# A two-block transformer kernel on one core: fewer extra matmuls, gates computed earlier, and one filler product moved

## The chip, the cores and the metric

The kernel runs on one core of one Trainium2 chip. The metric is the device time of one execution in microseconds (us), here the median of three runs.

## What is computed

256 tokens of width 1024 go through three layers, all in float32. The first two are a block with modulated norms: layer 0 mixes by Fourier transform and windowed attention, layer 1 by pooling, and each ends with a gated MLP of 22 hidden tiles of 128. The third layer is what the middle part of the change touches:

```python
h = rmsnorm(x, norm_mix)
(dn_qkv, dn_z, dn_b, dn_a, ns_q, ns_kc, ns_vc, ns_ks, ns_vs, ns_kw, ns_vw, ns_gate,
 gate_dn, gate_nsa) = split(h @ w_in)
...
beta = sigmoid(b_logit)
g = -exp(a_log) * softplus(a_logit + dt_bias)          # decay of the delta rule, per head
gates = sigmoid(gate_logits)                            # three branches of attention
...
mix = sigmoid(gate_dn) * (o_dn @ w_proj_dn) + sigmoid(gate_nsa) * (o_ns @ w_proj_nsa)
x = x + mix @ w_out
x = x + square(relu(rmsnorm(x, norm_mlp) @ w_up)) @ w_down
```

o_dn comes from the gated delta rule (8 heads, chunks of 64, a triangular solve for each), o_ns from attention over compressed, selected and windowed keys (16 heads of 64).

## The kernel before

**A product.** Every big product is `product(unit, xh, xl, ...)`. Weights and activations are split in a high part (float32r) and a low part, and each of the 8 slices of 128 rows of the contraction takes three matmuls of 256 columns: high by high (L562), high by low (L563), low by high (L564). One unit of weights (128 x 1024) is 24 matmuls, that is, eight such triples.

**Splitting the weights.** SyncE loads chunks into a ring. For each unit ScalarE (ACT) writes the high part (L1375, waiting for TensorE to be done with the unit four before), and VectorE (DVE) writes the low part (L1889, waiting for ACT's). Both do this inside their own copy of the order of work, up to three units ahead of TensorE (PE). In f1, `next_weights` takes the unit and the split of the unit ahead comes at the end of the same step.

**Order.** Each engine has its program written out by hand, and goes through it strictly in order. Waits are on named steps: `pe.at(step)`, `act.at(step)`, `dve.at(step)`.

**settle(x)** (L646) is one matmul of 128 x 64 on data already in place, into a scratch bank; its result is used by nobody. It stands at the end of each `opening`, at some steps j of the up phase of layers 0 and 1 (22 steps of two units), of the last MLP's up phase (32 steps of one unit, the first two in the opening), and at a few other places.

**f1** (third layer, projections for attention). PE: f1(12) to f1(15); `gates()`, a product for all small gate columns; f1(0); `gates_turned()`, two transposes; f1(1); f1(2) with `f1_squares(1)` behind its product (L580, which waits for ACT's squares L1627 of f1(0) and f1(1)); f1(3) with `f1_spread(1)` behind it (L953, which waits for DVE's reciprocal L2178 in its f1(3)); hidden(0), 64 matmuls for compressed keys; f1(4) and so on. On ACT, f1(j) is: for even j from 2 the deviation (a Sqrt, L1609), the square L1627, the copy L1629, the split of a unit ahead. On DVE it is: for odd j from 3 the reciprocal, and the split. `blocks(e)` on DVE (L2213) builds the input of hidden(e); `gates()` on DVE stands behind blocks(0), copies the turned gates to gt (L2148), and adds the bias to dt (L2150, L2151). `gates2()` on ACT (L1593 to L1599) waits for gt and dt and does two Tanh, Abs and two Exp; on DVE (L2157 to L2163) it finishes beta, gate and dt1. `gates3()` on ACT is a Ln of dt1 (L1603); on DVE it finishes gg.

**f2 and delta.** f2 is 24 products, and behind product s stand the steps `f2_later(s)` of the two before: DVE convolves along the tokens (L2400, L2403), ACT takes a Tanh (L1739), DVE multiplies (conv, L2391), PE transposes (L1143), ACT copies (L1730). So `f2_later(24)` and `f2_later(25)` are left over behind the last product. Behind `pe.note("f2")` and its likes the memory of the attention part is used anew, and the other engines wait there for each other. Then comes the delta rule: `decay(hd)` on PE (L1192 to L1194) waits for DVE's sources (L2443, L2444), ACT takes Exp (L1785), GpSimd masks (L2639), PE does `products(hd)` (L1200 to L1204), DVE multiplies (L2450 to L2458). 16 independent fillers (`fill()`; the first eight are one product each, the others two) stand between these steps. Behind the loop over hd come `level_first` (L1219) and the levels of the triangular solve.

Of the kernel before, what the change touches and what calls it, by code (L numbers as in the profile page):

```python
# [322 lines left out]
def program(nc, a):  # L323
    ctx = ExitStack()
    with ctx:
# [23 lines left out]
        pe, act, dve, pool = Mark(sem("s_pe")), Mark(sem("s_act")), Mark(sem("s_dve")), Mark(sem("s_pool"))  # L349
# [197 lines left out]
        def tensor_program(te):  # L547
# [280 lines left out]
            def swiglu(layer, norm, after):  # L828
                F.past(EXTRA[2][0])
                later = iter(ADA_LATER[layer])  # L830

                def ada_later():
                    of, _ = next(later)
                    F.used(F.raw(f"adaT{of}"))
                for j in range(NH0):
                    ps = take(RG, ("up", layer, j), (dve, ("prod", layer, j)))
                    if j == 0:
                        opening(f"w13_{layer}", norm, [(ps[:, 0:T], True), (ps[:, T:2 * T], False)], [("up", layer, 0, e) for e in range(2)])
                    for e in range(2 if j else 0):
                        u, _ = F.take(f"w13_{layer}")  # L840
                        product(u, xh, xl, norm, ps[:, e * T:(e + 1) * T]).then_inc(*pe.up(("up", layer, j, e), ("unit", u)))
                    if ADA_UP[layer](j):
                        ada_later()
                    if j in (1, 4, 8, 12, 16):
                        settle(xh)
                pe.note(("x", norm))
                n = 0
                for j in range(8):
                    ps = take(RG, ("down", layer, j), (dve, ("h", after, j)))
                    for k in range(NH0):  # L850
                        if n % 8 == 0:
                            u, _ = F.take(f"w2_{layer}")
                            _, hi, lo = unit_of(u)
                            P.wait_ge(*lo_done(u))
                        P.wait_ge(*dve.at("hid", layer, k))
                        c = slice((n % 8) * 128, (n % 8 + 1) * 128)
                        end = mm3(ps[:, 0:T], hi[:, c], lo[:, c], hh[:, k, :], hl[:, k, :], k == 0, k == NH0 - 1)
                        steps = [("unit", u)] * (n % 8 == 7) + [("down", layer, j)] * (k == NH0 - 1)
                        if steps:
                            end.then_inc(*pe.up(*steps))  # L860
                        if k == NH0 - 1 and j in (0, 3):
                            settle(hh)
                        if n % 8 == 7:
                            F.done(u)
                            if n % 16 == 15 and ADA_DOWN[layer](n // 16):
                                ada_later()
                        n += 1
                if layer == 0:
                    mean_square_rest(after)
                else:  # L870
                    mean_squares_last()
                pe.note(("hid", layer))
                if layer == 0:
                    spread(after)
# [253 lines left out]
            def f2_later(s):  # L1128

                if not 0 <= s - 2 < 24:  # L1130
                    return
                j = F2[s - 2]
                if j < 16 and j % 2:
                    ps = take(RAS, ("qks", j), (dve, ("qkv", j)))
                    for e in range(2):
                        P.wait_ge(*act.at("qksq", j - 1 + e))
                        end = column_sums(lambda t: ps[:, 2 * t + e:2 * t + e + 1], sq[:, j % 8 - 1 + e, :], 0, ones[:, 0:1])
                    end.then_inc(*pe.up(("qks", j)))
                if j >= 16:
                    P.wait_ge(*dve.at("conv", j))  # L1140
                    ps = take(RAS, ("vt", j), (act, ("vt", j)))
                    for t in range(2):
                        end = te.transpose(ps[:, t * 128:(t + 1) * 128], sq[:, j % 8, t * 128:(t + 1) * 128], ident)  # L1143
                    end.then_inc(*pe.up(("vt", j)))
# [3 lines left out]
            for s, j in enumerate(F2):  # L1148
                if STEPS2[s]:
                    attn_head(step)  # L1150
                u, _ = F.take("f2")
                ps = take(RGS, ("f2", j), (dve, ("f2", j)))
                product(u, xh, xl, "mix2", ps[:, 0:T]).then_inc(*pe.up(("f2", j), ("unit", u)))
                f2_later(s)
                if STEPS2[s]:
                    attn_tail(step)
                    step += 1


            def fill_z(j):  # L1160
# [13 lines left out]
            def fill(n=1):  # L1174
                for _ in range(n):
                    j = next(fillers)
                    if j < 8:
                        fill_z(j)
                    else:
                        gated("gn", j - 8, onh, onl, "on", RO)  # L1180


            fill()
            f2_later(24)
            f2_later(25)
            pe.note("f2")

            def decay(hd):
                ps = take(RA, ("decay", hd), (act, ("decay", hd)))
                P.wait_ge(*dve.at("rg", hd))  # L1190
# [16 lines left out]
            for hd in range(8):  # L1207
                if hd < 7:
                    decay(hd + 1)
                products(hd)  # L1210
                if hd in (1, 3, 5):
                    fill()

            def level_first(n):
# [117 lines left out]
            for j in range(2, NH2):  # L1332
                u, _ = F.take("up")
                ps = take(RG, ("mup", j), (act, ("mup", j)))
                product(u, xh, xl, "mlp2", ps[:, 0:T]).then_inc(*pe.up(("mup", j), ("unit", u)))
                if j in (2, 5, 9, 14, 20, 26):
                    settle(xh)
            n = 0
            for j in range(8):
# [17 lines left out]
        def scalar_program(sc):  # L1357
# [233 lines left out]
            def gates2():  # L1591
                A.wait_ge(*dve.at("gt"))
                sc.activation(beta[:, :, :], gt[:, :, 0:8], ACT.Tanh, scale=0.5).then_inc(*act.up("beta"))  # L1593
                sc.activation(gate[:, :, :], gt[:, :, 16:64], ACT.Tanh, scale=0.5).then_inc(*act.up("gate"))
                A.wait_ge(*dve.at("dt"))
                sc.activation(gw[:, 0, :, :], gt[:, :, 8:16], ACT.Abs).then_inc(*act.up())
                A.wait_ge(*act.now())
                sc.activation(gw[:, 0, :, :], gw[:, 0, :, :], ACT.Exp, scale=-1.0).then_inc(*act.up("dtexp"))
                sc.activation(ea[:, :], C("alog"), ACT.Exp).then_inc(*act.up("ea"))  # L1599

            def gates3():
                A.wait_ge(*dve.at("dt1"))
                sc.activation(gw[:, 1, :, :], gw[:, 1, :, :], ACT.Ln).then_inc(*act.up("dtln"))  # L1603
# [87 lines left out]
            for j in (12, 13, 14, 15):  # L1691
                f1(j)
            gates()
            for j in range(4):
                f1(j)
            gates2()
            gates3()
            hidden(0)
            f1(4)
            compressed(0)  # L1700
# [70 lines left out]
            def fill(n=1):  # L1771
                for _ in range(n):
                    j = next(fillers)
                    if j >= 8:
                        gated("gn", j - 8)
                        continue
                    weights("f3")
                    A.wait_ge(*pe.at("zz", j))
                    sc.activation(temp(("zz", j), (dve, ("zz", j))), ps_of(("zz", j))[:, 0:T], ACT.Tanh, scale=0.5).then_inc(*act.up(("zz", j)))
# [4 lines left out]
                    A.wait_ge(*dve.at("W", hd - 2))  # L1784
                sc.activation(Ebuf[:, hd % 2, :], ps_of(("decay", hd))[:, 0:384], ACT.Exp).then_inc(*act.up(("decay", hd)))  # L1785

            fill()
            decay(0)
            for hd in range(8):
                if hd < 7:  # L1790
                    decay(hd + 1)
                if hd in (1, 3, 5):
                    fill()
            fill()
            fill()
# [77 lines left out]
        def vector_program(ve):  # L1873
# [314 lines left out]
            def f1(j):  # L2188
                ahead = next_weights("f1")
                if j < 12 and j % 2 and j > 1:  # L2190
                    f1_inverse(j - 2)
                if j < 12 and j % 2 == 0 and j > 2:
                    unit_rms(j - 3)
                if j == 6:
                    compressed_keys()
                if j == 10:
                    compressed_values()
                split(ahead)
# [134 lines left out]
            f1(0)  # L2333
            blocks(0)
            gates()
            for j in (1, 2, 3):
                f1(j)
            gates2()
            gates3()
            V.wait_ge(*dve.at("qg"))  # L2340
            for half in range(2):
                F.used(F.raw("cw1"))
# [117 lines left out]

            sources(0)
            sources(1)
            fill()
            for hd in range(8):
                if hd < 6:
                    sources(hd + 2)
                products(hd)
                if hd in (1, 3, 5):
                    fill()

            fill()
# [467 lines left out]
```

## Time and profile before

| | us |
|---|---|
| median of three runs | 1208.61 |
| lowest and highest | 1206.75, 1209.2 |
| the profiled execution's own time | 1209.2 |
| its span, first to last instruction | 1207.4 |
| mean granted TensorE clock in it | 0.983 of full speed |
| PE, DVE, ACT, GpSimd busy | 1149.0, 814.4, 589.9, 81.8 |

The times of the profile count from the first instruction. A row of a timeline gives start, duration, engine, line, operation and how many were merged, and in brackets how long the engine was idle ahead of it and who released it. Matmuls overlap: the pace is read from start to start, not from the duration.

### The profile page before, as it was taken

The page shows a single profiled execution, that of the slowest core. Times are in us where ns is not written, and L with a number is a line of the kernel's source. Part 1 is how long each engine was busy: PE and PEld are TensorE (multiplying, and loading weights), DVE is VectorE, ACT ScalarE, POOL GpSimd, SP SyncE. Part 2 cuts the span into 40 slices and gives each one's busy share as a digit, 9 for nine tenths or more (in the row PEclk, how much of TensorE's full clock was granted, in tenths as well). Part 3 has the DMA queues.
Part 4 walks back from the last instruction along what each step waited for, and adds up shares of the span by engine and source line. Part 5 has one row for each costly group of instructions (what it writes and reads, how often), then busy time and mean ns, then how long its engine had stood idle before and what let it go on. Part 6 is the DMA issues. An engine that isn't in the chain of part 4 may idle for free.

```text
span 1207.4 us, 24317 instructions
## 1 busy us (share of the span) xinstructions
PE 1149.0 (95%) x10429; PEld 1092.4 (90%) x10429; DVE 814.4 (67%) x1490; ACT 589.9 (49%) x1084; POOL 81.8 (7%) x100
## 2 busy tenths in 40 slices
PE   5888789999998999999989999999999999999999
PEld 2687689999997999999989888888999999999999
DVE  3783668898886767555674678787664665877543
ACT  2434556454544545454465557653234445655432
POOL 0000110000011000001100111112600001000000
PEclk9789999999999999999998999999999999999999
DMA  9751548889884555751653232232123464855520
GB/s 388 291 207 60 215 170 329 334 340 349 320 328 174 222 222 223 255 187 43 246 175 105 106 105 80 97 105 71 38 72 106 157 211 159 323 198 185 208 84 14
DMA packets 32363, 226.41 MB, mean 188 GB/s; under 512 B 3584, under 2 KB 4736, under 8 KB 5120
## 3 DMA queue, kind: packets, MB, share of 16 engines
q1 hardware_dynamic: 30528, 221.20, 49.1%
q10 hardware_dynamic: 1728, 3.67, 0.8%
q8 instruction: 82, 1.34, 0.4%
q14 instruction: 25, 0.20, 0.1%
HBM read 223.80 MB, written 1.05 MB: 186 GB/s over the span
## 4 chain that ended last, share of the span: by engine, by line
PE 86%; DVE 8%; ACT 4%; DMA 1%; issue 1%; POOL 0%; SPq 0%; DVEq 0%; POOLq 0%
PE bank L562 23%; PE bank L563 22%; PE bank L564 22%; PE bank L1041 2%; PE bank L687 2%; DVE sb_tmp L1915 1%; DVE sb_ring L1930 1%; DVE sb_wlo L1889 1%; PE bank L580 1%; PE bank L1032 1%; PE bank L1063 1%; DMA sb_ring<-in_ada 1%; PE bank L590 1%; PE bank L600 1%; PE bank L1229 1%; PE bank L1247 1%
## 5 line engine op out<-in xcount | busy, mean ns | idle before, releaser
L562 PE MATMUL bank<-sb_xh,sb_whi 128*128 128x256 f32 x1488 | 422.9, 284 | 9.0 <-DVE sb_wlo L1889 6.7
L563 PE MATMUL bank<-sb_xl,sb_whi 128*128 128x256 f32 x1488 | 414.3, 278 | 0.0
L564 PE MATMUL bank<-sb_xh,sb_wlo 128*128 128x256 f32 x1488 | 414.3, 278 | 0.0
L1889 DVE TENSOR_TENSOR sb_wlo<-sb_ring,sb_whi 128x1024 fp32r<-128x1024 f32 (+1 forms) x197 | 239.1, 1220 | 138.5 <-ACT sb_whi L1375 138.1
L562 PEld LDWEIGHTS bank<-sb_xh,sb_whi 128*128 128x128 f32 x1488 | 281.6, 189 | 17.6 <-issue 12.8
L563 PEld LDWEIGHTS bank<-sb_xl,sb_whi 128*128 128x128 f32 x1488 | 282.2, 190 | 0.1
L564 PEld LDWEIGHTS bank<-sb_xh,sb_wlo 128*128 128x128 f32 x1488 | 281.7, 189 | 0.0
L1375 ACT ACTIVATE sb_whi<-sb_ring 128x1024 fp32r<-128x1024 f32 (+1 forms) x197 | 206.7, 1053 | 88.7 <-PE bank L564 81.3
L1889 DVE TENSOR_TENSOR sb_wlo<-sb_more,sb_whi 128x1024 fp32r<-128x1024 f32 x108 | 131.0, 1222 | 64.8 <-ACT sb_whi L1375 64.8
L562 PE MATMUL bank<-sb_hh,sb_whi 128*128 128x256 f32 x608 | 168.4, 277 | 0.0
L564 PE MATMUL bank<-sb_hh,sb_wlo 128*128 128x256 f32 x608 | 167.8, 276 | 0.0
L563 PE MATMUL bank<-sb_hl,sb_whi 128*128 128x256 f32 x608 | 167.8, 276 | 0.0
L1375 ACT ACTIVATE sb_whi<-sb_more 128x1024 fp32r<-128x1024 f32 x108 | 114.0, 1057 | 66.2 <-PE bank L564 56.1
L563 PEld LDWEIGHTS bank<-sb_hl,sb_whi 128*128 128x128 f32 x608 | 114.2, 188 | 0.0
L562 PEld LDWEIGHTS bank<-sb_hh,sb_whi 128*128 128x128 f32 x608 | 114.1, 188 | 0.0
L564 PEld LDWEIGHTS bank<-sb_hh,sb_wlo 128*128 128x128 f32 x608 | 114.1, 188 | 0.0
L1930 DVE CUSTOM_DVE_ANT_0 sb_ring<-sb_ring,sb_cB,sb_col 128x1024 f32<-128x1024 f32 x46 | 58.0, 1299 | 0.0
L1536 ACT ACTIVATE sb_tmp<-bank 128x256 f32<-128x256 f32 x44 | 16.9, 384 | 66.2 <-PE bank L564 66.2
L1397 ACT ACTIVATE sb_sq<-sb_h 128x256 f32<-128x256 f32 x48 | 19.2, 415 | 58.9 <-DVE sb_h L1944 54.2
L2600 POOL TENSOR_TENSOR sb_sq<-sb_sq 128x256 f32<-128x256 f32 x24 | 19.2, 801 | 367.2 <-ACT sb_sq L1397 366.3
L1930 DVE CUSTOM_DVE_ANT_0 sb_more<-sb_more,sb_cB,sb_col 128x1024 f32<-128x1024 f32 x34 | 42.7, 1292 | 0.0
L1667 ACT ACTIVATE sb_ss<-sb_ss,sb_st 128x128 f32<-128x128 f32 x64 | 28.1, 442 | 7.2 <-DVE sb_st L2303 7.2
(378 smaller groups left out, 1845.6 us busy)
## 6 DMA issues: line engine op xcount, KB each, us to landing
sb_more<-in_w SPq DMA_DIRECT2D x34, 1024.0 KB, 6.7
sb_ring<-in_w SPq DMA_DIRECT2D x32, 1024.0 KB, 6.0
sb_ring<-in_adaT SPq DMA_DIRECT2D x26, 1024.0 KB, 7.6
sb_ring<-in_f SPq DMA_DIRECT2D x22, 1024.0 KB, 5.0
sb_more<-in_adaT SPq DMA_DIRECT2D x18, 1024.0 KB, 9.5
sb_ring<-in_gn SPq DMA_DIRECT2D x8, 1024.0 KB, 4.9
sb_ring<-in_gd SPq DMA_DIRECT2D x8, 1024.0 KB, 4.9
sb_ring<-in_up SPq DMA_DIRECT2D x8, 1024.0 KB, 5.9
```

The source lines that it names most:

```text
L562: te.matmul(out, wh, rh, start=start, stop=False, skip_group_check=skip)
L563: te.matmul(out, wh, rl, start=False, stop=False, skip_group_check=skip)
L564: return te.matmul(out, wl, rh, start=False, stop=stop, skip_group_check=skip)
L687: end = te.matmul(ps_of(("row", e))[0:2, :], csil[:, k, :], w[:, o:o + 512], start=k == 0, stop=k == KT - 1)
L1041: end = te.matmul(ps[:, k * 128:(k + 1) * 128], ss[:, i % 3, u, k * 128:(k + 1) * 128], dg2[:, i % 2, 2 * u + (k > 0), :], start=True, sto ...
L1375: sc.activation(hi, x, ACT.Copy).then_inc(*hi_done.up(n))
L1397: sc.activation(sq[:, k, :], src[:, k, :], ACT.Square).then_inc(*act.up(("sq", norm, k)))
L1536: sc.activation(temp(("silu", layer, j), (dve, ("hid", layer, j))), ps_of(("up", layer, j))[:, 0:T], ACT.Silu).then_inc(*act.up(("silu", l ...
L1667: sc.activation(p, p, ACT.Exp, bias=x[:, 1, u, t:t + 1], scale=slope((2 * aa + u) * 4 + r), accum_out=x[:, 2, u, t:t + 1]).then_inc(*act.u ...
L1889: ve.tensor_tensor(lo, x, hi.bitcast(F32), ALU.subtract).then_inc(*lo_dve.up(n))
L1930: ve.tensor_tensor_reduce(out=x, in0=x, in1=cB[:, 0, :], scale=1.0, scalar=C(f"ab{layer}", jj, jj + 1), op0=ALU.mult, op1=ALU.add, accum_o ...
L2600: gp.tensor_tensor(sq[:, 0, :], sq[:, 0, :], sq[:, k, :], ALU.add).then_inc(*pool.up(("sum", norm, k)))
```

## The change

Four edits:

- PE leaves out the settle at j = 1, 4 and 12 in layers 0 and 1, and in the last up phase stands one at j = 11 and 21 in place of j = 2, 5, 9, 14, 20, 26.
- On all three engines the first filler, ahead of `decay(0)`, is taken out, and there is one more at hd = 7 of the delta loop. On PE the left-over `f2_later(24)` and `(25)` so follow the last f2 product directly.
- On ACT gates2 moves from behind f1(3) to behind f1(0), and gates3 to behind f1(1).
- On DVE gates2 moves to behind f1(1), and gates3 to behind f1(2).

```diff
@@ tensor_program, swiglu
-                    if j in (1, 4, 8, 12, 16):
+                    if j in (8, 16):
                         settle(xh)
@@ tensor_program, behind the f2 loop
+            f2_later(24)
+            f2_later(25)
+            pe.note("f2")
...
-            fill()
-            f2_later(24)
-            f2_later(25)
-            pe.note("f2")
@@ tensor_program, delta loop (the same in scalar_program and vector_program, which also lose the fill() ahead)
                 products(hd)
-                if hd in (1, 3, 5):
+                if hd % 2:
                     fill()
@@ tensor_program, last MLP
-                if j in (2, 5, 9, 14, 20, 26):
+                if j in (11, 21):
                     settle(xh)
@@ scalar_program, f1
             gates()
-            for j in range(4):
+            f1(0)
+            gates2()
+            f1(1)
+            gates3()
+            for j in (2, 3):
                 f1(j)
-            gates2()
-            gates3()
             hidden(0)
@@ vector_program, f1
             gates()
-            for j in (1, 2, 3):
-                f1(j)
+            f1(1)
             gates2()
+            f1(2)
             gates3()
+            f1(3)
```

## Rows read from the trace of the kernel before

**Rows 1.** The page, busy time, share of the span and instructions of each engine.

```profile
PE 1149.0 (95%) x10429; PEld 1092.4 (90%) x10429; DVE 814.4 (67%) x1490; ACT 589.9 (49%) x1084; POOL 81.8 (7%) x100
```

**Rows 2.** Waits of TensorE: line, releaser, us in total, times, longest.

```profile
PE bank L953 <- DVE sb_hdev L2178: 4.7, 4, 1.9
...
PE bank L1219 <- DVE sb_qk L2475: 0.2, 1, 0.2
```

**Rows 3.** Timeline of TensorE, around the settle at j = 1 in layer 0.

```profile
198.47 0.19 PE L649 MATMUL bank<-sb_xh 128*128 128x64 f32 x1
...
199.29 0.28 PE L562 MATMUL bank<-sb_xh,sb_whi 128*128 128x256 f32 x1
...
209.49 0.28 PE L562 MATMUL bank<-sb_xh,sb_whi 128*128 128x256 f32 x1
```

**Rows 4.** Timeline of TensorE, first and last of 91 matmuls without a break.

```profile
945.42 0.28 PE L562 MATMUL bank<-sb_xh,sb_whi 128*128 128x256 f32 x1
...
956.02 0.28 PE L562 MATMUL bank<-sb_onh,sb_whi 128*128 128x256 f32 x1
```

**Rows 5.** Timeline of VectorE, 600 to 615 us.

```profile
603.65 4.11 DVE L2213 TENSOR_TENSOR sb_bk<-sb_kcv,sb_col 64x240 f32<-64x240 f32 x8
...
608.20 0.16 DVE L2151 TENSOR_TENSOR sb_gt<-sb_gt,sb_col 128x8 f32<-128x8 f32 x1
...
610.68 0.20 DVE L2178 RECIPROCAL sb_hdev<-sb_hdev 128x8 f32<-128x8 f32 x1
612.13 1.23 DVE L1889 TENSOR_TENSOR sb_wlo<-sb_ring,sb_whi 128x1024 fp32r<-128x1024 f32 x1 [1.26 <-ACT sb_whi L1375]
...
614.19 0.17 DVE L2161 TENSOR_SCALAR sb_gw<-sb_gw 128x16 f32<-128x16 f32 x1
```

**Rows 6.** Timeline of ScalarE, 600 to 615 us.

```profile
601.41 1.06 ACT L1375 ACTIVATE sb_whi<-sb_qk 128x1024 fp32r<-128x1024 f32 x1
...
607.57 0.27 ACT L1609 ACTIVATE sb_hdev<-bank,sb_col 128x8 f32<-128x8 f32 x1 [1.90 <-PE bank L580]
607.73 0.38 ACT L1627 ACTIVATE sb_sq<-bank 128x256 f32<-128x256 f32 x1
...
608.26 1.07 ACT L1375 ACTIVATE sb_whi<-sb_ring 128x1024 fp32r<-128x1024 f32 x1
...
612.12 1.28 ACT L1593 ACT_TABLE_LOAD   x1
613.41 0.22 ACT L1593 ACTIVATE sb_beta<-sb_gt 128x16 f32<-128x16 f32 x1
...
614.06 0.19 ACT L1599 ACTIVATE sb_ea<-sb_col 128x8 f32<-128x8 f32 x1
```

**Rows 7.** Timeline of TensorE, 606 to 612 us.

```profile
606.58 0.95 PE L580 MATMUL bank<-sb_con,sb_sq 128*128 128x2 f32 x8
...
610.93 1.09 PE L953 MATMUL bank<-sb_con,sb_hdev 128*64 128x128 f32 x16 [0.47 <-DVE sb_hdev L2178]
```

**Rows 8.** TensorE by windows: us, busy (instructions), granted clock, DMA share, GB/s.

```profile
818.40:821.80 3.40, 2.93 (x10) 0.51 0.21 31
821.80:825.20 3.40, 3.40 (x23) 0.99 0.72 282
```

**Rows 9.** Timeline of TensorE, 812 to 819 us.

```profile
812.27 0.39 PE L562 MATMUL bank<-sb_xh,sb_whi 128*128 128x256 f32 x1
...
816.98 0.44 PE L1143 MATMUL bank<-sb_con,sb_sq 128*128 128x128 f32 x2 [1.48 <-DVE sb_sq L2391]
818.87 1.19 PE L1192 MATMUL bank<-sb_Msb,sb_con 128*128 128x256 f32 x2 [1.45 <-DVE sb_Msb L2444]
```

**Rows 10.** Timeline of VectorE, 812 to 815 us.

```profile
812.54 0.43 DVE L2391 SCALAR_TENSOR_TENSOR sb_sq<-sb_tmp,sb_sq 128x256 f32<-128x256 f32 x1 [2.37 <-ACT sb_tmp L1739]
...
813.40 1.51 DVE L2403 SCALAR_TENSOR_TENSOR sb_sq<-bank,sb_col,sb_sq 128x255 f32<-128x255 f32 x3
```

**Rows 11.** Timeline of ScalarE at 816 us.

```profile
816.05 0.41 ACT L1739 ACTIVATE sb_tmp<-sb_sq 128x256 f32<-128x256 f32 x1
```

More of the change, by code:

```diff
@@ L1785, in decay @@
                 sc.activation(Ebuf[:, hd % 2, :], ps_of(("decay", hd))[:, 0:384], ACT.Exp).then_inc(*act.up(("decay", hd)))
-            fill()
             decay(0)
@@ L1791, in scalar_program @@
                     decay(hd + 1)
-                if hd in (1, 3, 5):
+                if hd % 2:
                     fill()
@@ L2462, in vector_program @@
             sources(1)
-            fill()
             for hd in range(8):
@@ L2467, in vector_program @@
                 products(hd)
-                if hd in (1, 3, 5):
+                if hd % 2:
                     fill()
```

## The prediction

> **What bounds the kernel now.** The page comes first. TensorE (PE) is busy for 95% of the span [rows 1], so only three things can move the time: fewer or dearer matmuls, TensorE waiting, or its clock. The waits of TensorE come second: after the opening they are short, four waits on the reciprocal L2178 hold 4.7 us of them (the longest 1.9), and the level section behind the decay loop has 0.2 us [rows 2]. Third come the timelines of the three stretches that the diff touches: 190 to 220 us for the extra matmuls of settle, 600 to 618 us for the gates, 810 to 826 us for the start of the delta part. There the reader is to see who is late for whom.
>
> **Ten settle matmuls go.** They go at j = 1, 4, 12 in both layers, and six become two in the up phase: 3 + 3 + 4 = 10. The one at 198.47 is followed by triples that are back at their pace from 199.29, seven instructions later. From there to 209.49 lie 90 matmuls, so the pace is 0.1133 us each. Without the settle, the matmul that starts at 199.29 would start at 198.47 + 6 x 0.1133 = 199.15 [rows 3]. One settle thus costs 0.14 us, and ten give back 1.4 us. What a settle might buy shows elsewhere: at 945.42 to 956.02 the same triples, 90 matmuls, take 10.60 us, 0.1178 each [rows 4]. So there are two paces, 4.5 ns apart, and the slow one can last. But around 198 us the triples stand at the fast pace already ahead of the settle, and I found the same ahead of every settle that goes, so I take -1.4 us. The other end is the slow pace from the opening to the first settle kept: 7 x 48 matmuls in each layer and 9 x 24 in up, 888 x 4.5 ns = +4.0 us, less the 1.4.
>
> **The gates move earlier.** PE's own order stays: f1(0), the turned gates, f1(1), f1(2), squares(1), f1(3), spread(1), hidden(0). ScalarE (ACT) now does gates2 straight behind f1(0), and gates3 between f1(1) and f1(2). gates2 begins with a wait for gt, which VectorE (DVE) copies only after its eight operations of blocks(0), 603.65 to 607.76; the last of its gate inputs, dt, is there at 608.20 + 0.16 = 608.36 [rows 5]. ACT is free from 601.41 + 1.06 = 602.5 [rows 6], so it stands there with everything behind it: the square and the copy of f1(1), and the splits that DVE's halves wait for. Step by step:
>
> 1. gates2 on ACT takes 613.41 to 614.25, 0.84 us [rows 6], most of it before dt is used, so it ends at about 608.9. Its table load (1.28 us) lies inside the wait and costs nothing; if it did not, it would cost 1.3.
> 2. f1(1) on ACT: square, copy and split take 607.73 to 609.33 in the like f1(2), 1.60 us [rows 6]. So the square is done at 609.3 and the split at 610.5. PE's squares(1) need that square. They started at 606.58 [rows 7] and now start at 609.3: PE waits 2.7 us. Then f1(3) runs until about 613.0.
> 3. gates3 on ACT: the load for Ln, 1.28 us, to 611.8. Ln waits for dt1. DVE first has to do its half of f1(1)'s split (1.23 us, from 610.5) and then three operations of 0.17 [rows 5], which gives 612.2. Ln ends at 612.4.
> 4. f1(2) on ACT: now Sqrt needs its table back, 1.28 us, to 613.7. Then deviation, square, copy and split, 607.57 to 609.33, 1.76 us [rows 6], to 615.5.
> 5. DVE: its half of that split, 1.23 us, to 616.7; gates3, which I put at 0.4 from the small operations of 0.17; and then f1(3), which opens with the reciprocal, 0.20 us, done at 617.3. Before, it was done at 610.88 [rows 5].
>
> PE's spread(1) waits for that reciprocal. It starts at 617.3 in place of 610.93 [rows 7]: +6.4 us, in two idle pieces of 2.7 and 4.3 us (0.5 was there). In before all this ACT and DVE work lay beside hidden(0). What follows (hidden, blocks(1), squares(3), spread(3)) hangs on PE's own progress, so the delay is not made up. The table loads are as many as before, but two of them now lie on the path. DMA issues that wait for these splits move with them, by no more than PE does.
>
> The gates' low bound is 0: PE as now, if the copy of gt came before ACT needs it. I keep 6.4, since every step of the chain has a row. The high bound is two table loads that each carry as much again, +2.6.
>
> The rule that bears on steps 3 and 4 is in the Trainium skill, ScalarE: Activation LUTs, "What ACT_TABLE_LOAD costs": each switch of set costs a load of about 1283 ns and a drain of about 1380 ns. The load here is 1.28 us, but the drain doesn't show: ACT's load at 612.12 ends at 613.40 and its activation starts at 613.41 [rows 6]. By that page the sum would be 2.8 us higher than by the rows.
>
> **The clock.** Waits cost more than their length. Between 815.5 and 818.9 PE waited twice, 1.48 and 1.45 us [rows 9], and from 818.4 to 821.8 it was granted 0.51 of full speed, its 1.2 GHz level. It got through 10 matmuls there, against 23 in the 3.4 us behind [rows 8]. One such stretch takes half of PE's work in it, up to 1.7 us. The two new idle pieces each invite one. The first falls on f1(3), which has 4.3 us to spare. The second falls on spread(1) and hidden(0), where nothing covers it. I take +1.5 us, with bounds 0 and 3.4 (one more stretch).
>
> **The filler unit at the start of delta.** One product of 24 matmuls leaves 812.27 to 815.1 [rows 9] and comes back at hd = 7, at about 2.8 us of PE time. At its old place it covered DVE's conv and convolve. Without it PE comes to the transposes of f2_later(24) at 812.3 and finds conv done at 812.54 + 0.43 = 812.97. Then the last convolve ends at 814.9 whatever PE does [rows 10]. ACT's tanh, which sat behind copies of the late transposes until 816.05 [rows 11], can start at 814.95, which is 1.1 us earlier. The second transposes move from 816.98 to 815.9 and decay(0) from 818.87 to 817.8 [rows 9]. So PE gains 1.1 and owes the unit, 2.8: +1.7 us, if its new place covers no wait. Nothing is there to cover: the level section behind the loop waits 0.2 us in all [rows 2]. The bounds are +1.5 and +2.8 (nothing gained at the front). The clock already drops here. PE's idle time rises from 2.9 to nearly 5 us, so the half-speed stretch may begin earlier or last another: +0.3 taken, bounds -1.5 and +1.7. Removing fill from ACT and DVE ahead of decay(0) takes a split and a tanh out of their way; they are not late there.
>
> **Sum.** -1.4 + 6.4 + 1.5 + 1.7 + 0.3 = +8.5 us. The profiled execution took 1209.2 us, 1.8 more than its span of 1207.4, and would take 1217.7. The median of the three runs is 1208.6, so the forecast is 1217.1 us. About 0.2%, 2.4 us, is what a measurement of this kernel can tell from no change.
>
> **The rivals.**
> - The slow pace. The settles at j = 1 and 2 do cure something, and all three phases enter slowly and stay so. For it: rows 4 show 90 matmuls that never recover. Against it: the fast pace ahead of each settle that goes. 8.5 + 4.0 = +12.5, 1221.1 us. Chance 0.10.
> - Dear table switches: the two on the path carry as much again. Against it: the 0.01 us between load and activation [rows 6]. 8.5 + 2.6 = +11.1, 1219.7 us. Chance 0.05.
> - The gate chain is hidden anyway, so this part does nothing to PE: -1.4 + 1.7 + 0.3 = +0.6, 1209.2 us. It needs some 6 us of slack between ACT's f1(1) and PE's spread(1). Against it: PE already waited 0.47 us at that place [rows 7]. Chance 0.08.
> - Faster. The gates' small work leaves the place ahead of blocks(1), DVE gets to its reciprocals sooner, and PE's waits on L2178, 4.7 us [rows 2], go. That decides if gt is there before ACT needs it, about 604.1, and it comes 4 us later. +0.6 - 4.7 = -4.1, 1204.5 us. Chance 0.05.
> - The forecast: 0.72.
>
> **How the numbers follow.** The forecast's own range, from its bounds taken singly, is 1214 (no clock loss) to 1221 (one more slow stretch and a dearer delta). Taking in the slow pace and the dear tables gives 1213 to 1222, which leaves out the two cases at or under 1209 and the tails. Faster 0.05, same 0.08, slower 0.87.
>
> **What would show it.** Right: two new waits of PE, at L580 for ACT's square L1627 (about 2.7 us) and at L953 for L2178 (about 4.3); ACT's tanh for beta right behind 608 and loads for Ln and Sqrt between splits; a granted clock of 0.5 near 617 to 621; PE idle for about 5 us between the last f2 product and the first decay; no wait less behind hd = 7; 19 matmuls of settle in place of 29; and layer and up phases each shorter by 0.4 to 0.6 us. Wrong: the first wait of L953 as short as before, the triples at 0.118 us between opening and first settle, or a level section that starts with less delay than the unit is long.

## The result, and the profile after

| | before | after |
|---|---|---|
| median, us (9 runs each) | 1209.20 | 1217.56 |
| lowest to highest, us | 1206.73 to 1213.06 | 1212.56 to 1221.59 |
| profiled execution, us (its span) | 1209.2 (1207.4) | 1213.92 (1212.1) |

The ratio is 1.0058, with a 95% interval of 1.0039 to 1.0079: 4.7 to 9.6 us slower. The change made the kernel slower; 1217.1 was forecast.

The profiled execution after is only 4.7 us longer than the one of before. The missing part has nothing to do with the change: everything ahead of layer 0's MLP took 180.19 us in place of 185.94. TensorE waited about as long there in both: 14.0 us for the first chunk from DMA before and 14.6 after, and 21.1 and 20.8 us in all behind that. But it was granted half the clock for 27.3 us of that stretch before, and for 17.1 after. Most of the difference lies between the first matmul and the first triple: 34.7 us at a mean granted clock of 0.78 before, 28.3 us at 0.93 after. Over all the profiles below the stretch took 180.2 to 187.0 us. So the parts are compared by stretches, from one named matmul to the next:

| stretch of TensorE, us | before | after | difference |
|---|---|---|---|
| layer 0, opening to the sums behind down | 182.15 | 181.73 | -0.42 |
| layer 1, the same | 181.39 | 180.97 | -0.42 |
| turned gates (L932) to first spread (L953) | 10.17 | 16.28 | +6.11 |
| first to second spread | 13.35 | 14.58 | +1.24 |
| second spread to first scores | 39.66 | 38.48 | -1.18 |
| first scores to the levels | 190.43 | 192.34 | +1.91 |
| last MLP, opening to the end | 176.20 | 176.69 | +0.49 |

The -1.18 is the clock's: before had 5.9 us at half speed there, after had 3.4, and e2, e3 and e7 below, with no edit there, show -1.0 to -1.2 as well. Two stretches without an edit are longer after: from the sums behind layer 0 to layer 1's opening (+0.95) and from layer 1 to the turned gates (+1.81). In each of them after has a stretch at half the clock (from 373.61 and from 574.99 us) where before has none; e1 and e7 show both increases too. The edited parts sum to 8.9 us, and with these four unedited ones (-5.75, +0.95, +1.81, -1.18) that gives the 4.7 of the profiles.

The page's first line after answers to rows 1: TensorE is still the bound.

```profile
PE 1148.2 (95%) x10419; PEld 1094.8 (90%) x10419; DVE 814.4 (67%) x1490; ACT 590.2 (49%) x1084; POOL 81.9 (7%) x100
```

The waits of TensorE after answer to rows 2. Lines behind the edits lie one to three lower than before: L2176 is the reciprocal L2178 of before, L1624 ScalarE's square L1627, L1189 the first matmul of a decay.

```profile
PE bank L953 <- DVE sb_hdev L2176: 6.8, 4, 2.7
PE bank L1143 <- DVE sb_sq L2390: 3.1, 2, 2.4
...
PE bank L580 <- ACT sb_sq L1624: 2.1, 1, 2.1
...
PE bank L1189 <- DVE sb_Msb L2443: 1.4, 1, 1.4
```

The wait of 2.1 us at L580 is new, those at L953 grew by 2.1, and those at L1143 doubled.

**The gates, link by link.** ScalarE's timeline after (against rows 6; subtract 596.93 here and 600.76 there, the turned gates, to compare times):

```profile
598.65 1.28 ACT L1590 ACT_TABLE_LOAD   x1
604.23 0.22 ACT L1590 ACTIVATE sb_beta<-sb_gt 128x16 f32<-128x16 f32 x1 [4.29 <-DVE sb_gt L2146]
...
604.97 0.36 ACT L1624 ACTIVATE sb_sq<-bank 128x256 f32<-128x256 f32 x1
...
605.50 1.06 ACT L1372 ACTIVATE sb_whi<-sb_ring 128x1024 fp32r<-128x1024 f32 x1
606.57 1.28 ACT L1600 ACT_TABLE_LOAD   x1
608.13 0.21 ACT L1600 ACTIVATE sb_gw<-sb_gw 128x16 f32<-128x16 f32 x1 [0.27 <-DVE sb_gw L2159]
608.36 1.28 ACT L1606 ACT_TABLE_LOAD   x1
609.66 0.27 ACT L1606 ACTIVATE sb_hdev<-bank,sb_col 128x8 f32<-128x8 f32 x1
```

VectorE's in the same stretch (against rows 5):

```profile
599.81 4.06 DVE L2211 TENSOR_TENSOR sb_bk<-sb_kcv,sb_col 64x240 f32<-64x240 f32 x8
603.90 0.29 DVE L2146 COPY sb_gt<-bank 128x128 f32<-128x128 f32 x1
...
606.59 1.23 DVE L1887 TENSOR_TENSOR sb_wlo<-sb_ring,sb_whi 128x1024 fp32r<-128x1024 f32 x1 [1.98 <-ACT sb_whi L1372]
...
607.93 0.17 DVE L2159 TENSOR_SCALAR sb_gw<-sb_gw 128x16 f32<-128x16 f32 x1
...
611.45 1.23 DVE L1887 TENSOR_TENSOR sb_wlo<-sb_ring,sb_whi 128x1024 fp32r<-128x1024 f32 x1 [3.27 <-ACT sb_whi L1372]
...
612.95 0.20 DVE L2176 RECIPROCAL sb_hdev<-sb_hdev 128x8 f32<-128x8 f32 x1
```

And TensorE's, which waits at both ends of it (against rows 7):

```profile
602.75 0.50 PE L580 MATMUL bank<-sb_con,sb_sq 128*128 128x2 f32 x4
605.39 0.75 PE L580 MATMUL bank<-sb_con,sb_sq 128*128 128x2 f32 x4 [2.14 <-ACT sb_sq L1624]
613.21 1.98 PE L953 MATMUL bank<-sb_con,sb_hdev 128*64 128x128 f32 x16 [2.75 <-DVE sb_hdev L2176]
```

ScalarE idles 4.29 us until gt is there, with the table already loaded. Its square comes 8.0 us behind the turned gates in place of 3.3 (before, it started at 604.06), TensorE's second half of squares(1) waits for it, and from there the chain goes back and forth: split, VectorE's half, dt1 at 607.93, Ln, load, root, split, VectorE's half at 611.45, reciprocal at 612.95. The two loads (ACT_TABLE_LOAD, which brings in the table of a function) at 606.57 and 608.36 lie on it.

**The clock.** TensorE by windows after (columns as in rows 8):

```profile
602.30:605.70 3.40, 1.26 (x13) 1.00 0.50 212
605.70:609.10 3.40, 3.40 (x17) 0.50 0.00 0
609.10:612.50 3.40, 1.36 (x12) 1.00 0.00 0
612.50:616.00 3.50, 2.79 (x28) 0.51 0.00 0
...
817.30:824.10 6.80, 4.84 (x16) 0.50 0.00 0
```

Each of the two new idle pieces comes with a stretch at the 1.2 GHz level. The first falls on f1(3), the second on spread and hidden(0), and at the start of delta the half-speed stretch is 6.8 us long, against 3.4 before [rows 8].

This does not go with every wait. The same wait of 2.2 us stands in all twelve profiles behind layer 0, before:

```profile
378.60 0.39 PE L562 MATMUL bank<-sb_whi,sb_xh 128*128 128x256 f32 x1 [2.16 <-ACT sb_z L1565]
```

and after:

```profile
372.44 0.39 PE L562 MATMUL bank<-sb_whi,sb_xh 128*128 128x256 f32 x1 [2.17 <-ACT sb_z L1562]
```

Before, the clock stayed full behind it. After, the windows show 0.50 from 373.60 on. Four of the twelve profiles (after, e2, e6, e10) have a half-speed stretch at this wait, eight have none. The wait of 1.8 to 1.9 us ahead of the second spread has none in any of the nine profiles that have the wait. What decides it was not found.

**The start of delta** after (against rows 9): three waits of 0.68, 2.42 and 1.45 us, where there were two of 1.48 and 1.45.

```profile
814.96 0.44 PE L1143 MATMUL bank<-sb_con,sb_sq 128*128 128x128 f32 x2 [0.68 <-DVE sb_sq L2390]
817.81 0.69 PE L1143 MATMUL bank<-sb_con,sb_sq 128*128 128x128 f32 x2 [2.42 <-DVE sb_sq L2390]
819.95 0.77 PE L1189 MATMUL bank<-sb_Msb,sb_con 128*128 128x256 f32 x1 [1.45 <-DVE sb_Msb L2443]
```

**The settles.** The layers came out as forecast, the last MLP didn't. These are its triples behind the opening, up to the first settle that is left, at j = 11:

```profile
1039.24 0.28 PE L562 MATMUL bank<-sb_xh,sb_whi 128*128 128x256 f32 x1
...
1067.04 0.28 PE L564 MATMUL bank<-sb_xh,sb_wlo 128*128 128x256 f32 x1
1067.16 0.20 PE L649 MATMUL bank<-sb_xh 128*128 128x64 f32 x1
```

Between the first two rows lie 236 steps in 27.80 us: 0.1178 us each, the slow pace of rows 4. Behind the settle it is 0.1133. Here the slow start did happen, and it cost 240 x 4.5 ns = 1.1 us. It began right behind the settle that closes the opening (at 1038.11) and a wait of 0.49 us, so that settle did not keep it off.

### The profile page after: what moved, and what is told of

Same layout as the page of the kernel before. It is cut to its first block, busy times and chain, and to the rows that moved or that the text cites. A ratio compares the mean times of both kernels' runs of the same rounds, so it can differ in the third digit from the quotient of the medians.

```text
span 1212.1 us, 24299 instructions
## 1 busy us (share of the span) xinstructions
PE 1148.2 (95%) x10419; PEld 1094.8 (90%) x10419; DVE 814.4 (67%) x1490; ACT 590.2 (49%) x1084; POOL 81.9 (7%) x100
## 4 chain that ended last, share of the span: by engine, by line
PE 86%; DVE 8%; ACT 4%; DMA 1%; issue 1%; POOL 0%; SPq 0%; DVEq 0%; POOLq 0%
PE bank L562 23%; PE bank L563 22%; PE bank L564 22%; PE bank L1041 2%; PE bank L687 1%; DVE sb_tmp L1913 1%; DVE sb_wlo L1887 1%; DVE sb_ring L1928 1%; PE bank L580 1%; DMA sb_ring<-in_ada 1%; PE bank L1032 1%; ACT sb_whi L1372 1%; PE bank L1063 1%; PE bank L600 1%; PE bank L1226 1%
## 5 line engine op out<-in xcount | busy, mean ns | idle before, releaser
L562 PEld LDWEIGHTS bank<-sb_xh,sb_whi 128*128 128x128 f32 x1488 | 283.2, 190 | 17.1 <-issue 12.4
L2630 POOL TENSOR_TENSOR sb_dg<-sb_con,sb_st 128x512 f32<-128x512 f32 x16 | 17.6, 1098 | 209.9 <-DVE sb_st L2309 209.9
```

The lines of the kernel that those rows point to most:

```text
L562: te.matmul(out, wh, rh, start=start, stop=False, skip_group_check=skip)
L2630: gp.tensor_tensor(dg2[:, i % 2, :, :], ident.unsqueeze(1).to_broadcast([128, 4, 128]), x, ALU.mult).then_inc(*pool.up(("dg2", i)))
```

## The experiments

Medians and ratios are against runs of the kernel before on the same chip. Where the time can't tell, the stretches of the profile do: stretches without an edit, a change of clock or a change of pace mostly repeat within 0.1 us from kernel to kernel, many within 0.02.

### One edit alone

**e1_gates**: only the two reorderings of gates2 and gates3.

> Only the gates edit is made, on ScalarE and VectorE; settles and fillers stay as in the kernel before. If the cause is the chain behind gt (ScalarE stands at gates2 until VectorE has done blocks(0)), TensorE waits about 2.1 to 2.7 us at L580 and about 4 us (less what the half clock takes into f1(3)) at the first L953, from the turned gates to the first spread it takes 16.3 us in place of 10.2, and the time is 6 to 9 us above the kernel before. If the settles or the filler carried the loss and the gates' order cost nothing, the time is within 2 us of before and the stretch from the turned gates to the first spread stays at 10.2 us.

Measured: 1216.8 against 1209.16, ratio 1.0060 (1.0039 to 1.0081). Turned gates to first spread 16.28 us, first to second spread 14.59, new wait at L580 2.2 us, longest at L953 2.7. The edit alone gives the whole loss, within the interval: 7.3 us. In the profile it is 6.12 + 1.25 = 7.4 us, the second number being the half clock on spread(1) and hidden(0).

**e2_fill**: only the filler moved.

> Only the filler is moved, from ahead of decay(0) to hd = 7. If the cover at the old place was real and nothing is covered at the new one, TensorE waits about 0.7 and 2.4 us at L1143 and again ahead of decay(0), last f2 product to decay(0) takes 9.7 us in place of 10.6, decay(0) to the level section 33 to 34 in place of 30.2, and the time rises by 1.7 to 3. If the moved product hides a wait at its new place, the second stretch grows by less than 2 us and the time stays within 1 us.

Measured: 1211.55, ratio 1.0015 (0.9993 to 1.0036), which by itself is no proof. First scores to levels 192.39 us in place of 190.43, +2.0. The three profiles with the filler moved (after, e2, e4) have 192.1 to 192.4 us here, the seven with it at its old place 190.0 to 190.4. The waits are 0.7, 2.4 and 1.4 us as in the kernel after, and decay(0) to the level section is 34.22 us in place of 30.17. The new place covers nothing: the level section's own stretch is 0.35 us shorter, and that is all.

**e3_settle**: only the ten settles gone.

> Only the ten settles go. If a settle is no more than its own 0.14 us, each layer's stretch from opening to the end of down is 0.42 us shorter, the last MLP 0.56 us, and the time falls by 1.4, which the runs can hardly tell. If the triples can enter a phase at the slow pace of 0.1178 us and stay there until the next settle, as in the last MLP of the changed kernel, some phase shows 0.1178 from its opening to its first settle, and costs 1.0 us (last MLP) or 1.6 us (a layer) more; the sum is then between -1.4 and +2.8.

Measured: 1207.09, ratio 0.9984 (0.9964 to 1.0004), which is no proof by itself. Layer stretches -0.43 and -0.43, last MLP -0.55: 0.14 us for each settle, and here no phase started slow.

**e5_no_settle**: all settles in the three up phases gone.

```diff
-                    if j in (1, 4, 8, 12, 16):
+                    if j in ():
...
-                if j in (2, 5, 9, 14, 20, 26):
+                if j in ():
```

> The kernel before with no settle left in the up phases of the two layers and of the last MLP (those in the openings and in the down phases stay): 10 + 4 + 2 = 16 go. If a settle costs 0.14 us and the pace is set once, when a phase starts, a layer's stretch is 0.7 us shorter and the last MLP 0.84, unless a phase starts slow: then it stays at 0.1178 us up to the settle in down, 3.9 us more for the last MLP and 4.7 for a layer. If the slow pace cures itself within a few units, no phase is longer than before.

Measured: 1206.21, ratio 0.9977 (0.9962 to 0.9992). The stretches are 0.70, 0.69 and 0.84 us shorter, again 0.14 for each settle; all three phases started fast and stayed so to their end. It does not tell how long a slow start would last in this kernel.

### The gate chain cut at different links

**e4_gt_first**: the whole change, but gt is made before blocks(0).

```diff
             f1(0)
-            blocks(0)
             gates()
+            blocks(0)
             f1(1)
```

> The whole change, but VectorE does gates() ahead of blocks(0), so gt is there about 4 us sooner. If the wait for gt starts the chain, the wait at L580 goes (the square of f1(1) is done ahead of it), and the reciprocal that the first spread waits for comes some 2 us sooner than in the changed kernel, near 14 us behind the turned gates: VectorE still does blocks(0), two halves of splits, gates2 and gates3 ahead of it, and ScalarE two table loads. The time is 2 to 4 us under the changed kernel. If the table loads alone made the chain, the first spread starts as late as in the changed kernel (16 us behind the turned gates) and the time does not fall.

Measured: 1216.91, ratio 1.0063 (1.0041 to 1.0084). The first half came out: the wait at L580 is gone, and the first spread starts 14.25 us behind the turned gates. The time did not fall. TensorE's one wait is now longer:

```profile
PE bank L953 <- DVE sb_hdev L2176: 8.6, 4, 4.5
```

From 609.3 to 616.1 the clock was at half, and the stretch to the second spread grew to 15.77 us in place of 14.58. So 1.2 of the 2.0 us won at the first spread were lost to the clock: the two stretches together take 30.02 us, against 30.86 in the changed kernel and 23.52 in the kernel before. The 0.8 us that is left is less than the medians can tell (1216.91 and 1217.56). The next stretch, to the first scores, was 40.02 us with two half-speed stretches, but e5, with no edit anywhere near, shows 39.99.

**e9_ln_back**: e1, but gates3 left behind f1(3).

```diff
             f1(0)
             gates2()
-            f1(1)
+            for j in (1, 2, 3):
+                f1(j)
             gates3()
-            for j in (2, 3):
-                f1(j)
...
             f1(2)
+            f1(3)
             gates3()
-            f1(3)
```

> The gates edit of e1, but gates3 (the Ln and what follows it) stays behind f1(3) on both engines. If the load for Ln and the wait for dt1 lie on the chain, the first spread starts about 2 us sooner than in e1: near 14.2 us behind the turned gates in place of 16.3. If only the wait for gt counts, it stays at 16.3. The rest of f1 may pay some of it back, since gates3 then lies ahead of blocks(1) again.

Measured: 1211.92, ratio 1.0021 (0.9998 to 1.0044). TensorE in that stretch (the turned gates were at 603.64):

```profile
609.47 0.50 PE L580 MATMUL bank<-sb_con,sb_sq 128*128 128x2 f32 x4
612.12 0.61 PE L580 MATMUL bank<-sb_con,sb_sq 128*128 128x2 f32 x4 [2.15 <-ACT sb_sq L1627]
617.79 0.44 PE L953 MATMUL bank<-sb_con,sb_hdev 128*64 128x128 f32 x4 [0.60 <-DVE sb_hdev L2179]
```

The first spread comes at 14.14 us, as expected, and the first wait is as long as in e1. So gates3 in the middle, with its load and its wait for dt1, is worth 2.1 us; the load for Sqrt stays on the chain here (613.31). With the second wait down to 0.6, hidden(0) also ran at full clock (the next stretch is 13.25 us), so that the profile has the two stretches 3.5 us shorter than in e1. The medians differ by 4.9, with intervals that overlap.

**e10_gates_inverse**: e1 with VectorE's reciprocals taken one step earlier (the edit of e6, below).

> The gates edit of e1 with the earlier reciprocals of e6. The last links of the chain are then cut out: the reciprocal no longer stands behind ScalarE's square, copy and split of f1(2), VectorE's half of that split and gates3, but follows the square root. If the chain is as I laid it out, the first spread starts about 3 us sooner than in e1, near 13 us behind the turned gates; the first wait, at L580, stays as long as in e1. If the square root itself is the last thing to be late by more than I think, the spread comes no sooner.

Measured: 1212.27, ratio 1.0000 (0.9969 to 1.0031), with e6's own gain in it. VectorE had the reciprocal ready 13.0 us behind the turned gates (600.95), which is where the chain puts it:

```profile
613.99 0.20 DVE L2180 RECIPROCAL sb_hdev<-sb_hdev 128x8 f32<-128x8 f32 x1 [1.79 <-ACT sb_hdev L1609]
```

But TensorE came to its spread later still, at 14.75 us, and without any wait:

```profile
609.42 1.01 PE L580 MATMUL bank<-sb_con,sb_sq 128*128 128x2 f32 x4 [2.15 <-ACT sb_sq L1627]
...
615.70 1.14 PE L953 MATMUL bank<-sb_con,sb_hdev 128*64 128x128 f32 x16
```

```profile
609.00:612.40 3.40, 2.98 (x14) 0.50 0.00 0
612.40:615.80 3.40, 3.40 (x18) 0.50 0.00 0
```

The matmuls of f1(3) ran at half clock. Once the chain is shorter, what is left of the delay is the first wait and the clock that it met. With the early reciprocals in both kernels, the gates edit still costs 5.2 us by the profiles: the two stretches take 26.19 us here and 21.03 in e6. The medians and the ratio are wide here (its interval spans 7.5 us), so this rests on the stretches.

### Changes the other way

**e6_inverse**: the kernel before, and f1_inverse(j - 1) done in the even f1 step.

```diff
-                if j < 12 and j % 2 and j > 1:
-                    f1_inverse(j - 2)
+                if j in (2, 4, 8, 10):
+                    f1_inverse(j - 1)
                 if j < 12 and j % 2 == 0 and j > 2:
                     unit_rms(j - 3)
                 if j == 6:
                     compressed_keys()
+                    f1_inverse(j - 1)
```

> The kernel before with VectorE's reciprocal for the spreads of 1, 3, 5, 7 and 9 taken one step earlier, into the even f1 step. If those spreads wait only because the reciprocal stands behind other work of VectorE, the waits at L953 fall from 4.7 us to under 1 and the time falls by 3 to 4 us. If ScalarE's square roots are what is late, the waits stay.

Measured: 1204.84, ratio 0.9978 (0.9959 to 0.9996): 2.7 us faster. All waits at L953 are gone. The first two were worth 0.54 and 1.94 us, about as long as they were (0.47 and 1.87). Of the later ones, new waits of 0.4 us at L580 and of 1.4 at the next consumer took a part:

```profile
PE bank L1010 <- DVE sb_nq L2186: 1.4, 1, 1.4
```

**e7_fill_two**: the kernel before, with a second fill() on all three engines ahead of decay(0), taken from hd = 1.

```diff
             f2_later(25)
             pe.note("f2")
+            fill()
...
-                if hd in (1, 3, 5):
+                if hd in (3, 5):
                     fill()
```

> The opposite of the filler edit: the kernel before with a second filler between the last transposes and decay(0), taken from hd = 1. If TensorE's idle time and low clock there are what a filler covers, the wait of 1.45 us ahead of decay(0) goes, and most of the 1.5 us that the low clock took; the stretch from the last transposes to the level section is 2 to 3 us shorter and the time falls as much. If decay(0) and what follows were the bound, the stretch stays as long as it was.

Measured: 1205.1, ratio 0.9974 (0.9955 to 0.9993). TensorE at the start of delta (L1193 is the decay here):

```profile
814.07 0.44 PE L1143 MATMUL bank<-sb_con,sb_sq 128*128 128x128 f32 x2 [1.48 <-DVE sb_sq L2393]
...
817.08 0.59 PE L1193 MATMUL bank<-sb_Msb,sb_con 128*128 128x256 f32 x2
...
821.05 0.67 PE L1193 MATMUL bank<-sb_Msb,sb_con 128*128 128x256 f32 x2 [0.74 <-DVE sb_Msb L2446]
```

decay(0) starts without a wait and the clock stays at full. But the third decay now waits 0.74 us for its source and the next two 0.1 and 0.2, and the stretch from the last transposes to the level section is 1.4 us shorter (30.68 for 32.06), less than I expected. The ratio says 3.1 with an interval from 0.8 to 5.4, so the two don't contradict each other.

**e8_both**: e6, e7, and settle only at j = 1 of a layer and j = 2 of the last MLP.

> e6 and e7 together, and settle only at j = 1 of each layer's up phase and at j = 2 of the last one (13 fewer than before, where a slow start is cured early). If the parts add up, 4 + 2.5 + 1.8 us come off the kernel before: about 1201 us against 1209. If the low clock or a new wait takes the gains back, it is within 3 us of before.

Measured: 1198.62 against 1208.58, ratio 0.9934 (0.9909 to 0.9959): 8.0 us faster than the kernel before and, by the two ratios, some 15 (1209.2 x 0.0124) faster than the changed one. Each part is in the profile as in its own run: settles -0.57, -0.55 and -0.61, the two spreads -0.54 and -1.94, delta -1.4. They sum to 5.6 us, inside the interval of the ratio (5.0 to 11.0) but under its middle; what is missing is not traced to an edit. The last MLP did start slow here, and behind the settle at j = 2, after one unit, it ran at the fast pace.

## Why the prediction was right

The mechanism was right: the gates carry the loss, the filler adds to it, the settles give a little back. The size (8.5 forecast, 8.4 by the medians, 7.0 by the ratio, 8.9 by the edited stretches) agrees as well, though that the absolute time came out within 0.5 us of 1217.1 is luck: the interval is 5 us wide, and the settles missed by 1.0. By parts:

- **Settles: -1.4 forecast, -0.35 found.** 0.14 us each holds to the second digit in e3 and e5. In the changed kernel's profile it was -0.42 in each layer but +0.49 in the last MLP, since the rival of the slow pace came true in one of the three phases, for 1.1 us; triples at 0.118 us there were among the signs named for being wrong. I gave it 0.10 for all three. Over the twelve profiles here the last MLP started slow three times (after, e7, e8), the layers never. It is a part that comes and goes, and it does not decide the sign.
- **Gates: +6.4 forecast, +6.1 found.** Each link is in the rows: gates2 ends 8.1 us behind the turned gates (forecast 8.1), dt1 is there at 11.2 (11.4), the reciprocal is done at 16.2 (16.5). e1 shows that the edit alone does it, e9 that gates3 in the middle is 2.1 us of it, e10 that the last links are as laid out. What was off is the split into two waits, 2.1 and 2.7 in place of 2.7 and 4.3: half of squares(1) could already run, and the clock took f1(3) from 2.8 to 4.2 us from first to last start, inside the slack that I had named.
- **Clock: +1.5 forecast, +1.2 found** on spread(1) and hidden(0), at the place named. e4 and e10 show that it can be more: there it took back a part of what the shorter chain had won. That a new wait would bring a half-speed stretch held in all five kernels with the gates edit. It was not certain from before: of the waits that all kernels share, one has such a stretch in some profiles only, another in none.
- **Filler: +1.7 and +0.3 forecast, +1.9 found**, in e2 +2.0. The front (last f2 product to decay(0)) gained 0.9 in place of 1.1, and the half-speed stretch lasted 6.8 us in place of 3.4.
- **Table loads.** Neither load on the chain shows a drain. The first ends at 606.57 + 1.28 = 607.85 and the Ln starts at 608.13, right behind the dt1 that it waits for. The reload at 608.36 ends at 609.64, with the root at 609.66. By the Trainium skill, ScalarE: Activation LUTs, "What ACT_TABLE_LOAD costs", a drain of about 1380 ns belongs to each switch; the trace disagrees here too.
- **The other rivals.** That the chain would be hidden fell with e1. The faster rival had its mechanism right, VectorE's reciprocals being late by order alone, but the change doesn't touch that order in its favour: e6 does, and gains 2.7.

## What to carry to other kernels

Before moving a small chain of operations forward on an engine that works in order, find when its input is ready and what stands behind it there: here a copy behind 4 us of other work held up a weight split on one engine, its second half on the other, and then TensorE. Price a wait of TensorE with a stretch at half clock as a risk, not as a certainty: it came with all the waits that the gates edit added (2.1 to 4.5 us), but a wait of 2.2 us elsewhere, the same in all kernels, had one with it in four profiles of twelve. For the same reason, compare single profiles by stretches, and look at the granted clock before explaining a difference. Independent fillers belong where the engine is about to wait; where nothing waits, they cover nothing and cost their own time.

## What had not been expected

The same sequence of matmuls runs at 0.1133 or at 0.1178 us each, at full granted clock. In the last MLP of the changed kernel the slow pace lasted for 236 steps, until another kind of matmul came between. In all three profiles where the last MLP started slow, a matmul of 128 x 64 was followed by the fast pace (after: at 1067.16; e7 and e8: behind the first unit). But such a matmul is no sure cure. One stands in all twelve kernels in the output projection ahead of the last MLP, behind its first unit, and in e1, e3 and e5 the slow pace begins right behind it (e1):

```profile
1013.55 0.19 PE L649 MATMUL bank<-sb_mxh 128*128 128x64 f32 x1
...
1015.31 0.28 PE L564 MATMUL bank<-sb_mxh,sb_wlo 128*128 128x256 f32 x1
...
1033.33 0.28 PE L564 MATMUL bank<-sb_mxh,sb_wlo 128*128 128x256 f32 x1
```

Between the last two rows lie 153 steps in 18.02 us, 0.1178 each; in the other nine profiles the same steps take 17.34 us, 0.1133 each. No edit touches that place. In all twelve the unit ahead of it runs at the fast pace, up to two longer steps of about 0.2 us shortly before the settle. So which pace a sequence gets differed between kernels that have the same instructions there. What sets it was not found.
